# Two more modulation blocks in layer 0's second feed-forward sweep, none in layer 1's recurrent sweeps

## The chip, the cores and the metric

The kernel runs on one core of one Trainium2 chip. The metric is the device time of the whole program in microseconds (us); lower is better. A core has a matrix engine (PE), two elementwise engines (DVE and ACT), GpSimd (POOL) and a queue engine (SP) that here does nothing but start the loads of weights.

## What is computed

One inference step of a two-layer network on 128 context tokens and 128 latent tokens with 2048 channels, everything in float32. Layer 0 mixes by attention, layer 1 by a recurrent block; a feed-forward part (8192 wide, squared ReLU) follows each. Every sub-layer is normalised before and after, and shifted, scaled and gated by values that come from the two condition vectors through one linear map per layer:

```python
def adaln(cond, w, b):
    m = jax.nn.silu(cond) @ w + b
    return [t[:, None, :] for t in jnp.split(m, 6, axis=-1)]
...
    for layer in range(DEPTH):
        shm_p, scm_p, gm_p, shf_p, scf_p, gf_p = adaln(ctx_cond, w_ada[layer], b_ada[layer])
        shm_s, scm_s, gm_s, shf_s, scf_s, gf_s = adaln(c, w_ada[layer], b_ada[layer])
        hp = rmsnorm(yp, g_pre_mix[layer]) * (1 + scm_p) + shm_p
...
        yp = yp + gm_p * rmsnorm(op, g_post_mix[layer])
        hp = rmsnorm(yp, g_pre_ffn[layer]) * (1 + scf_p) + shf_p
...
        yp = yp + gf_p * rmsnorm(ffn(hp, w_ff1[layer], w_ff2[layer]), g_post_ffn[layer])
```

`w_ada` is 2 x 2048 x 12288. In blocks of 512 columns each layer has 24: 0 to 3 the shift and 4 to 7 the scale ahead of the mixer, 8 to 11 the mixer's gate, 12 to 15 the shift and 16 to 19 the scale ahead of the feed-forward part, 20 to 23 its gate. The change is about blocks 12 to 19 of layer 1.

## The kernel before

All weights are streamed once from memory in tiles of 512 rows by 512 columns (1 MB each). There are two kinds of tile. An M tile belongs to one of the big products; ACT and DVE split it into a rounded part (`w_hi`, L776) and the rest (`w_lo`, L1027), in two halves, and PE multiplies both parts with the activations. An A tile belongs to the modulation map; PE takes it as it is (L494, 8 recorded matmuls), and four A tiles make one modulation block.

The work is a list of sweeps (`plan`, L64). Each sweep runs a number of iterations, and each iteration goes through a string of M and A by which SP loads and PE multiplies. Those that matter here: `ff2_0` (layer 0's second feed-forward product) runs 4 iterations of `"MMA" * 4 + "M" * 8`; `rec_in_a` and `rec_in_b` (the recurrent block's input product) and `rec_out` (its output product) run 4 iterations of `"MA" * 4` each; `ff1_1` follows without A tiles. The A tiles of `rec_in_b` and `rec_out` are blocks 12 to 15 and 16 to 19 of layer 1.

All tiles pass through one ring of four slots, `raw`. SP starts the loads strictly in the order of the strings (`tiles`, L361). The load for a position waits until the tile four positions earlier is out of its slot: an M tile is out when DVE has made its `w_lo`, an A tile when PE has multiplied it (`released`, L319).

A modulation block ends in four steps. After its fourth A tile DVE adds the bias, and splits the sum into a short and a long part (`ada_rows_out`: L1061, L1063, L1065); the bank that holds the sum is one for all blocks, so PE's first A tile of the next block waits for this (`ada_row`, in `ada_tile`, L486). Then PE turns the row into columns (L514) or spreads it over the partitions (L518) in `ada_end`, and DVE stores the result (`ada_store`: L1075 for columns, L1079 for a gate). POOL loads each block's bias, and a gate's gain.

In most sweeps (skew) these steps stand in the next iteration: `ada_rows_out` behind the second half of its first M tile. `ff2_0` and `ff2_1` do them within the iteration, `ada_rows_out` behind half 19, which is the tenth M tile's second half, two M tiles after the fourth A tile (halves are numbered from 0: half 19 belongs to the tenth M tile).

In `rec_in_b` the engines do more beside the product. For each of four chunks in an iteration PE computes the recurrence's gates (`rg_gates`, L556), ACT their tanh and exp (L826 to L830), DVE the coefficients and scans (L1324 to L1343); after four chunks ACT takes a square root (L837), ahead of which no scan of these chunks can start. Behind `rec_in_b` DVE finishes the last scans while PE begins `rec_out`, whose fourth M tile needs the last of them.

Of the kernel before, what the change touches and what calls it, by code (L numbers as in the profile page):

```python
# [48 lines left out]
class Sweep:  # L49


    def __init__(self, name, n, mode, weight, col0, tiles, blocks, ada, ada_at, order, out, skew=True):
# [3 lines left out]
        self.ada, self.ada_at = ada, ada_at  # L56
# [4 lines left out]
        assert order.count("M") == tiles * blocks and len(order) % NRAW == 0  # L61


def plan(w):  # L64

    ma = "MA" * 4
    sweeps = [
        Sweep("ada0", 8, None, None, 0, 0, 0, "cols", (0, 0), "AAAA", None),
        Sweep("att_in_a", 4, "token", w["att_in"], 0, 4, 1, "gate", (0, 8), ma, "qkv"),
        Sweep("att_in_b", 5, "token", w["att_in"], 4, 4, 1, "cols", (0, 12), ma, "qkv"),  # L70
        Sweep("att_out_a", 3, "token", w["att_out"], 0, 4, 1, "cols", (0, 17), ma, "op"),
        Sweep("att_out_b", 1, "token", w["att_out"], 3, 4, 1, None, None, "MMMM", "op"),
        Sweep("ff1_0", 8, "feature", w["ff1_0"], 0, 4, 2, "cols", (1, 0), "MMA" * 4, "hidden"),
        Sweep("ff2_0", 4, "token", w["ff2_0"], 0, 16, 1, "gate", (0, 20), "MMA" * 4 + "M" * 8, "op", False),
        Sweep("rec_in_a", 4, "feature", w["rec_in"], 0, 4, 1, "gate", (1, 8), ma, "xr"),
        Sweep("rec_in_b", 4, "feature", w["rec_in"], 4, 4, 1, "cols", (1, 12), ma, "gr"),
        Sweep("rec_out", 4, "token", w["rec_out"], 0, 4, 1, "cols", (1, 16), ma, "op"),
        Sweep("ff1_1", 8, "feature", w["ff1_1"], 0, 4, 2, None, None, "M" * 8, "hidden"),
        Sweep("ff2_1", 4, "token", w["ff2_1"], 0, 16, 1, "gate", (1, 20), "MMA" * 4 + "M" * 8, "op", False),
    ]  # L80
    pos = half = ada = token = feature = gate = main = 0
    for s in sweeps:

        s.pos0, s.main0, s.half0, s.ada0, s.token0, s.feature0, s.gate0 = pos, main, half, ada, token, feature, gate
        pos += s.n * len(s.order)
        main += s.n * s.order.count("M")
        half += s.n * s.halves
        ada += s.n * bool(s.ada)
        gate += s.n * (s.ada == "gate")
        if s.mode == "token":  # L90
            token += s.n * s.blocks
        if s.mode == "feature":
            feature += s.n * s.blocks
    return sweeps


def hybrid_step(nc, A, out):
# [26 lines left out]
    with ctx:  # L124
# [80 lines left out]
        state_rows = rpb[0:2 * KC, 0, :]  # L205
        CONV_W, CONV_B, B_A, B_X, LAM, H0 = 0, 64, 80, 112, 144, 176
# [100 lines left out]
        NORM_ADA = {0: 8, 1: 20, 2: 28, 3: 44}  # L307
# [11 lines left out]
        def released(s, it, p):  # L319


            if p >= NRAW:
                at, upto = (s, it), p - NRAW + 1
            elif first(it):
                k = sweeps.index(s)
                if k == 0:
                    return None
                b = sweeps[k - 1]
                at, upto = (b, b.n - 1), len(b.order) - NRAW + p + 1
            else:  # L330
# [4 lines left out]
            return ada_used, TILE * b.ada0 + i * b.order.count("A") + b.order[:upto].count("A")  # L335
# [23 lines left out]
        @block.sync  # L359
        def _(sp):  # L360
            def tiles(s, it, before):  # L361
                m = a = 0
                for p, kind in enumerate(s.order):
                    if kind == "M":
                        b, t = divmod(m, s.tiles)
                        w, col = s.weight[t], (s.col0 + it * s.blocks + b) * BLK
                        m += 1
                    else:
                        layer, col0 = s.ada_at
                        w, col = W_ada[layer][a], (col0 + it) * BLK  # L370
                        a += 1
                    if not isinstance(it, int):
                        col = sp.snap(col)
                    free = released(s, it, p)
                    if free:
                        sp.wait_ge(*free)
                    sp.dma_start(raw[:, p % NRAW, :, :], w[:, :, bass.ds(col, BLK)]).then_inc(raw_landed[p % NRAW], 16)

            sp.dma_start(stage[0:96, 0, :], A["vectors"][0:96, :]).then_inc(vec_a_landed, 16)
            sp.dma_start(ident[:, :], A["ident"]).then_inc(id_landed, 16)  # L380
            sp.dma_start(sel[:, :], A["sel"]).then_inc(id_landed, 16)
            for s in sweeps:
                iterations(sp, s, tiles, None)
# [3 lines left out]
        def _(pool):  # L387
            def ada_loads(s, it, before):

                b = s.ada0 + it  # L390
                layer, col = s.ada_at
                if not isinstance(b, int) or b > 0:
                    pool.wait_ge(ada_row, b)
                src = A["b_ada"][layer:layer + 1, bass.ds((col + it) * BLK, BLK)]
                pool.dma_start(bias_rows[0:2 * NG, :], src.broadcast_to([2 * NG, BLK])).then_inc(bias_landed, 16)  # L395
                if s.ada == "gate":
                    name = "g_post_ffn" if col >= 20 else "g_post_mix"
                    pool.wait_ge(ada_fin, b)
                    src = A[name][layer:layer + 1, bass.ds(it * BLK, BLK)]
                    pool.dma_start(gain_rows[:, :], src.broadcast_to([P, BLK])).then_inc(gain_landed, 16)  # L400
# [67 lines left out]
            iterations(pool, S["rec_out"], ada_loads, None)  # L468
# [16 lines left out]
        def _(pe):  # L485
            def ada_tile(s, it, p, a):  # L486

                slot, landed = stream(s, it, p)
                b = s.ada0 + it
# [14 lines left out]
            def ada_end(s, it):  # L504

                b = s.ada0 + it
# [5 lines left out]
                if s.ada == "cols":  # L512
# [47 lines left out]
            def body(s, it, before):  # L560
                lanes = NG if s.mode == "token" else BLK // P
                m = a = 0
                for p, kind in enumerate(s.order):
                    if kind == "A":
                        if not (first(it) and p < s.ada_early):
                            ada_tile(s, it, p, a)
                        a += 1
                        if s.mode is None and a == 1 and before and before[0].ada:
                            ada_end(*before)
                        continue  # L570
# [41 lines left out]
                    if m == (3 if s.out == "gr" else 2) and before and before[0].ada and before[0].skew:  # L612
# [133 lines left out]
            ada_end(*last)  # L746
# [3 lines left out]
            ada_end(*last)  # L750
# [262 lines left out]
        def _(dve):  # L1013
# [39 lines left out]
            def ada_rows_out(s, it):  # L1053


                b = s.ada0 + it
# [11 lines left out]
            def ada_store(s, it):  # L1068
                b = s.ada0 + it
                dve.wait_ge(ada_small, b + 1)  # L1070
                if s.ada == "cols":

                    base = s.ada_at[1] - (12 if s.ada_at[1] >= 12 else 0)
                    flat = ada_cols[:, :, :, :].rearrange("p a c g -> p (a c g)")
                    V.tensor_copy(flat[:, bass.ds((base + it) * 4 * NG, 4 * NG)], ps[5][:, 0:4 * NG]).then_inc(ada_fin, 1)  # L1075
# [6 lines left out]
            def body(s, it, before):  # L1082
# [5 lines left out]
                for b in range(s.blocks):  # L1088
                    last = (s, it * s.blocks + b - 1) if b else (before and (before[0], before[1] * before[0].blocks + before[0].blocks - 1))
                    for hh in range(2 * s.tiles):  # L1090
# [22 lines left out]
                        if before and before[0].ada and before[0].skew and b == 0:  # L1113
# [4 lines left out]
                        if not s.skew and hh == 19:  # L1118
                            ada_rows_out(s, it)
                        if not s.skew and hh == 25:  # L1120
                            ada_store(s, it)

            def gate_of(s, blk):

                return {"att_out_a": 12, "att_out_b": 12, "ff2_0": S["ff2_0"].ada0 + blk + 1,
# [41 lines left out]
            def norm(n, gain, ahead, h0):  # L1167
# [3 lines left out]
                steps(V.scalar_tensor_tensor(out=gs, in0=ada_cols[:, 1], scalar=1.0,  # L1171
# [9 lines left out]
                for j in range(KC // 2):  # L1181
# [3 lines left out]
                    for c in range(2):  # L1185
                        for g in range(NG):
                            at = (c * NG + g) * T
                            e = V.tensor_scalar(h_mod[:, j % 2, c, g, :], ps[NORM_BANKS[j % 3]][:, at:at + T],
                                                gs[:, 2 * j + c, g:g + 1], ada_cols[:, 0, 2 * j + c, g:g + 1],
# [239 lines left out]
            ada_rows_out(*last)  # L1429
            split_early("rec_out", 2, 4)  # L1430
            gelu_arguments(3)
            ada_store(*last)
# [14 lines left out]
            ada_rows_out(*last)  # L1447
            dve.wait_ge(states_turned, 1)
            V.tensor_copy(state_rows, ps[6][0:2 * KC, 0:P]).then_inc(state_rows_ready, 1)
            ada_store(*last)  # L1450
# [61 lines left out]
```

## Time and profile before

| | |
|---|---|
| time, 3 runs | median 2509.38 us (2508.92 to 2511.56) |
| span of the profiled execution | 2507.5 us |
| PE busy in it | 2356.4 us (94%) |
| DVE, ACT busy | 1492.8 us (60%), 1107.1 us (44%) |
| SP's loads of weights | 574.77 MB, 65.5% of the 16 DMA engines' span |

The span runs from the first to the last instruction of that execution, so its own time is at least the span; the page gives no more of it. The time on the chip stands some 2 us over it (2509.38 against 2507.5). PE's records overlap, as one matmul starts before the one ahead has drained, so the share of busy time is no measure of how full PE is; better is the distance from one start to the next. The profile's chain of waits follows the run back from its last instruction, at each step to whatever released it, and names the engine and line that the time belongs to.

### The profile page before, as it was taken

The numbers are of one execution on the slowest core, as the hardware profiler recorded it, in microseconds if no ns is written. First come the engines' busy times: TensorE is split into PE (matmuls) and PEld (weight loads), VectorE is DVE, ScalarE is ACT, GpSimd is POOL, SyncE is SP. The second block draws the span as 40 slices with busy tenths as digits, with TensorE's granted clock in tenths as the row PEclk, the third lists the DMA queues.
The fourth block names the chain that finished last, engine by engine and source line by source line (L and its number), as shares of the span: only waits on it lengthen the run. The fifth ranks groups of instructions, "written<-read, shape, count | busy, mean of one in ns | idle before, by whom it ended". The sixth has DMA issues, their size and how long they took to land.

```text
span 2507.5 us, 34322 instructions
## 1 busy us (share of the span) xinstructions
PE 2356.4 (94%) x12179; PEld 1818.1 (73%) x12179; DVE 1492.8 (60%) x2055; ACT 1107.1 (44%) x1529; POOL 85.9 (3%) x139
## 2 busy tenths in 40 slices
PE   5799997989999999999998999897999999999996
PEld 1366765668888887877876777665888888777775
DVE  2444445456555556666767668865655556666665
ACT  0132334334333334555554358733444444555553
POOL 1000000000000000000000011000000000000000
PEclk8799998989999999999999999998999999999998
DMA  9989880765777777666674887687455555766763
GB/s 355 330 299 323 308 316 5 276 227 189 252 251 252 250 251 258 225 250 214 223 251 150 304 285 246 240 284 274 152 189 184 196 186 178 258 220 212 249 218 117
DMA packets 296342, 592.14 MB, mean 236 GB/s; under 512 B 11569, under 2 KB 11825, under 8 KB 296017
## 3 DMA queue, kind: packets, MB, share of 16 engines
q1 hardware_dynamic: 289744, 574.77, 65.5%
q0 software_dynamic: 6528, 16.46, 2.1%
q8 instruction: 42, 0.69, 0.1%
q14 instruction: 28, 0.22, 0.0%
HBM read 587.76 MB, written 3.42 MB: 236 GB/s over the span
## 4 chain that ended last, share of the span: by engine, by line
PE 86%; DMA 5%; DVE 4%; ACT 2%; issue 1%; POOL 1%; DVEq 0%; SPq 0%; ACTq 0%; POOLq 0%
PE bank L539 22%; PE bank L529 15%; PE bank L531 14%; PE bank L530 14%; PE bank L541 11%; PE bank L494 6%; DMA raw<-in_w_ada 3%; PE bank L644 1%; PE bank L556 1%; PE bank L678 1%; DMA raw<-in_w_rec_in 1%; DVE w_lo L1027 1%; DVE x L1154 1%; DMA raw<-in_w_att_in 1%; POOL small L405 0%
## 5 line engine op out<-in xcount | busy, mean ns | idle before, releaser
L1027 DVE TENSOR_TENSOR w_lo<-raw,w_hi 128x1024 fp32r<-128x1024 f32 x712 | 858.0, 1221 | 512.4 <-ACT w_hi L776 511.0
L776 ACT ACTIVATE w_hi<-raw 128x1024 fp32r<-128x1024 f32 x712 | 734.0, 1051 | 725.9 <-DMA raw<-in_w_att_in 217.9
L539 PE MATMUL bank<-xt,w_hi 128*128 128x512 f32 x2560 | 907.5, 399 | 4.0 <-DVE R L1047 2.5
L541 PE MATMUL bank<-xt,w_lo 128*128 128x256 f32 x2560 | 713.4, 279 | 0.0
L529 PE MATMUL bank<-w_hi,xt 128*128 128x512 f32 x1568 | 624.9, 399 | 11.8 <-DVE w_lo L1027 4.1
L531 PE MATMUL bank<-w_hi,xt 128*128 128x512 f32 x1568 | 612.1, 390 | 0.0
L530 PE MATMUL bank<-w_lo,xt 128*128 128x512 f32 x1568 | 611.7, 390 | 0.0
L539 PEld LDWEIGHTS bank<-xt,w_hi 128*128 128x128 f32 x2560 | 480.4, 188 | 159.2 <-issue 31.9
L541 PEld LDWEIGHTS bank<-xt,w_lo 128*128 128x128 f32 x2560 | 481.9, 188 | 0.4
L529 PEld LDWEIGHTS bank<-w_hi,xt 128*128 128x128 f32 x1568 | 294.9, 188 | 150.5 <-issue 66.5
L531 PEld LDWEIGHTS bank<-w_hi,xt 128*128 128x128 f32 x1568 | 295.0, 188 | 63.4
L530 PEld LDWEIGHTS bank<-w_lo,xt 128*128 128x128 f32 x1568 | 295.4, 188 | 58.8 <-issue 0.5
L1025 DVE TENSOR_TENSOR xt<-R,xt 128x512 fp32r<-128x512 f32 x256 | 176.8, 690 | 234.5 <-ACT w_hi L776 234.1
L775 ACT ACTIVATE xt<-R 128x512 fp32r<-128x512 f32 x256 | 161.3, 630 | 315.0 <-PE bank L531 188.0
L494 PE MATMUL bank<-raw,cond 128*32 128x512 f32 x1536 | 225.9, 665 | 31.1 <-DVE ada_rows L1065 16.1
L494 PEld LDWEIGHTS bank<-raw,cond 128*32 128x32 f32 x1536 | 31.9, 112 | 113.2 <-issue 56.8
L812 ACT ACTIVATE R<-bank 128x256 f32 (+1 forms) x160 | 59.8, 381 | 110.3 <-PE bank L541 110.1
L1047 DVE TENSOR_TENSOR R<-bank,R 128x256 f32 (+1 forms) x160 | 65.9, 420 | 33.1 <-ACT R L812 32.7
L395 POOL DMA_DIRECT2D bias_rows<-in_b_ada x48 | 24.6, 513 | 1705.4 <-DVE ada_rows L1065 1705.4
L1061 DVE TENSOR_TENSOR ada_sum<-bank,bias_rows 128x512 f32<-128x512 f32 x48 | 32.9, 686 | 73.0 <-PE bank L494 73.0
L644 PE MATMUL bank<-R,x 128*128 128x128 f32 x256 | 40.8, 323 | 34.3 <-DVE R L1164 34.3
L644 PEld LDWEIGHTS bank<-R,x 128*128 128x128 f32 x256 | 38.7, 237 | 38.6 <-DVE R L1164 25.2
(171 smaller groups left out, 916.1 us busy)
## 6 DMA issues: line engine op xcount, KB each, us to landing
raw<-in_w_ff SPq DMA_DIRECT2D x256, 1024.0 KB, 5.4
raw<-in_w_ada SPq DMA_DIRECT2D x192, 1024.0 KB, 5.6
raw<-in_w_att_in SPq DMA_DIRECT2D x36, 1024.0 KB, 7.0
raw<-in_w_rec_in SPq DMA_DIRECT2D x32, 1024.0 KB, 7.0
raw<-in_w_att_out SPq DMA_DIRECT2D x16, 1024.0 KB, 7.2
raw<-in_w_rec_out SPq DMA_DIRECT2D x16, 1024.0 KB, 7.2
gain_rows<-in_g_post_mix POOLq DMA_DIRECT2D x8, 256.0 KB, 5.0
gain_rows<-in_g_post_ffn POOLq DMA_DIRECT2D x8, 256.0 KB, 4.1
```

What stands on the lines that cost most here:

```text
L494: mm = nc.tensor.matmul(ps[4][32 * j:32 * j + 32, :], cond[:, TILE * a + j, :], raw[:, slot, j, :], start=(a == 0), stop=(a == TILE - 1))
L529: nc.tensor.matmul(o, hi, w_hi[:, h, k, :], start=(begin and k == 0), stop=False)
L530: nc.tensor.matmul(o, hi, w_lo[:, h, k, :], start=False, stop=False)
L531: mm = nc.tensor.matmul(o, lo, w_hi[:, h, k, :], start=False, stop=(end and k == 1))
L539: nc.tensor.matmul(ps[m][:, :], w_hi[:, h, k, m * P:(m + 1) * P], xt[:, c, :], start=(begin and k == 0), stop=False)
L541: mm = nc.tensor.matmul(ps[m][:, 0:NG * T], w_lo[:, h, k, m * P:(m + 1) * P], xt[:, c, 0:NG * T], start=False, stop=(end and k == 1))
L644: mm = nc.tensor.matmul(ps[NORM_BANKS[j % 3]][:, at:at + T], x[:, g, (2 * j + c) * P:(2 * j + c + 1) * P], diag[:, g, :], start=True, stop ...
L775: nc.scalar.activation(xt[:, c:c + 2, 0:NG * T], hidden[:, 2 * h:2 * h + 2, :], ACT.Copy)
L776: nc.scalar.activation(w_hi[:, h % NSPLIT, :, :], raw[:, slot, 2 * q:2 * q + 2, :], ACT.Copy)\
L1025: V.tensor_tensor(xt[:, c:c + 2, NG * T:2 * NG * T], hidden[:, 2 * h:2 * h + 2, :], xt[:, c:c + 2, 0:NG * T].bitcast(fp32), ALU.subtract)
L1027: V.tensor_tensor(w_lo[:, h % NSPLIT, :, :], raw[:, slot, 2 * q:2 * q + 2, :], w_hi[:, h % NSPLIT, :, :].bitcast(fp32), ALU.subtract).then ...
L1047: V.tensor_tensor(dst, ps[m][:, 0:NG * T], dst, ALU.add).then_inc(chunk_read, 1)
```

## The change

A sweep can now have several modulation blocks in an iteration. `ff2_0` gets three: the gate block that it had, then two shift or scale blocks for layer 1's feed-forward part (columns 12, 14, 16, 18 as second and 13, 15, 17, 19 as third block of the four iterations). Its string becomes `"MA" * 8 + "MAA" * 2 + "M" * 6`. `rec_in_b` and `rec_out` lose theirs and become `"MMMM"`. Since layer 1's mixer columns are still in use at that time, the new blocks are stored in the space of `window`, a table that only the attention reads; the norm ahead of `ff1_1` reads them there.

```diff
+        at = [i for i, kind in enumerate(order) if kind == "A"][TILE - 1::TILE]
+        self.ada_after = [order[:i].count("M") for i in at]
...
     ma = "MA" * 4
+    two = "MMA" * 4 + "M" * 8
+    three = "MA" * 8 + "MAA" * 2 + "M" * 6
...
-        Sweep("ff2_0", 4, "token", w["ff2_0"], 0, 16, 1, "gate", (0, 20), "MMA" * 4 + "M" * 8, "op", False),
-        Sweep("rec_in_a", 4, "feature", w["rec_in"], 0, 4, 1, "gate", (1, 8), ma, "xr"),
-        Sweep("rec_in_b", 4, "feature", w["rec_in"], 4, 4, 1, "cols", (1, 12), ma, "gr"),
-        Sweep("rec_out", 4, "token", w["rec_out"], 0, 4, 1, "cols", (1, 16), ma, "op"),
+        Sweep("ff2_0", 4, "token", w["ff2_0"], 0, 16, 1,
+              [("gate", 0, 20, 1), ("cols", 1, 12, 2), ("cols", 1, 13, 2)], three, "op", False),
+        Sweep("rec_in_a", 4, "feature", w["rec_in"], 0, 4, 1, [("gate", 1, 8, 1)], ma, "xr"),
+        Sweep("rec_in_b", 4, "feature", w["rec_in"], 4, 4, 1, [], "MMMM", "gr"),
+        Sweep("rec_out", 4, "token", w["rec_out"], 0, 4, 1, [], "MMMM", "op"),
...
+        ffn_cols = window[:, 0:2 * KC * NG].rearrange("p (a c g) -> p a c g", a=2, g=NG)
...
-        NORM_ADA = {0: 8, 1: 20, 2: 28, 3: 44}
+        NORM_ADA = {0: 8, 1: 20, 2: 28, 3: 40}
...
-                    if not s.skew and m == 11:
-                        ada_end(s, it)
+                    if not s.skew:
+                        for k, after in enumerate(s.ada_after):
+                            if m == after + 3:
+                                ada_end(s, it, k)
...
-                        if not s.skew and hh == 19:
-                            ada_rows_out(s, it)
-                        if not s.skew and hh == 25:
-                            ada_store(s, it)
+                        if not s.skew:
+                            for k, after in enumerate(s.ada_after):
+                                if hh == 2 * after + 3:
+                                    ada_rows_out(s, it, k)
+                                if hh == 2 * after + 9:
+                                    ada_store(s, it, k)
```

On PE the calls of `ada_end` behind `rec_in_b` and behind `rec_out` go, on DVE those of `ada_rows_out` and `ada_store` there, on POOL the bias loads of the two sweeps (`ff2_0` has them instead). For `ff2_0` the rule `ada_after` gives 4, 8 and 10 M tiles, so `ada_rows_out` stands behind halves 11, 19 and 23.

On SP, the queue of loads in `ff2_0`'s first iteration (`in_w_ff` are M tiles, `in_w_ada` A tiles; a load waits for `lo_ready` where an M tile leaves its slot, for `ada_used` where an A tile does). Before, from the iteration's fourth and last A tile to its end:

```order
L377 DMA raw<-in_w_ada 128x4x512 [waits lo_ready]
L377 DMA raw<-in_w_ff 128x4x512 [waits ada_used]
L377 DMA raw<-in_w_ff 128x4x512 [waits lo_ready] x2
L377 DMA raw<-in_w_ff 128x4x512 [waits ada_used]
L377 DMA raw<-in_w_ff 128x4x512 [waits lo_ready] x4
```

With the change, from the ninth M tile to the fourteenth:

```order
L397 DMA raw<-in_w_ff 128x4x512 [waits lo_ready]
L397 DMA raw<-in_w_ada 128x4x512 [waits ada_used]
L397 DMA raw<-in_w_ada 128x4x512 [waits lo_ready]
L397 DMA raw<-in_w_ff 128x4x512 [waits ada_used]
L397 DMA raw<-in_w_ada 128x4x512 [waits lo_ready]
L397 DMA raw<-in_w_ada 128x4x512 [waits ada_used]
L397 DMA raw<-in_w_ff 128x4x512 [waits ada_used]
L397 DMA raw<-in_w_ff 128x4x512 [waits lo_ready]
L397 DMA raw<-in_w_ff 128x4x512 [waits ada_used] x2
```

The first row is the ninth M tile and the fourth row the tenth; the tenth's load now waits until PE has used the A tile four positions earlier, the eighth of the iteration.

On PE, the end of the fifth M tile of `ff2_0`'s first iteration and what follows. Before, the sixth M tile comes at once:

```order
L529 MATMUL bank<-w_hi,xt 128x512
L530 MATMUL bank<-w_lo,xt 128x512
L531 MATMUL bank<-w_hi,xt 128x512
L529 MATMUL bank<-w_hi,xt 128x512 [waits lo_ready]
L530 MATMUL bank<-w_lo,xt 128x512
```

With the change, at the end of the ninth M tile (behind the fifth it reads the same with one A tile in place of two):

```order
L552 MATMUL bank<-w_hi,xt 128x512
L515 MATMUL bank<-raw,cond 32x512 [waits ada_row,raw_landed1]
L515 MATMUL bank<-raw,cond 32x512 x3
L515 MATMUL bank<-raw,cond 32x512 [waits raw_landed2]
L515 MATMUL bank<-raw,cond 32x512 x3
L550 MATMUL bank<-w_hi,xt 128x512 [waits lo_ready]
```

The first A tile of a new block now stands between M tiles and waits for DVE's `ada_row`; the tenth M tile is queued behind it.

On DVE, in the same iteration, what stands ahead of that `ada_row` (the second block's), with the change:

```order
L1046 TENSOR_TENSOR xt<-R,xt 128x2x256 [waits hi_ready]
L1048 TENSOR_TENSOR w_lo<-raw,w_hi 128x1024
L1082 TENSOR_TENSOR ada_sum<-bank,bias_rows 128x512 [waits ada_small,bias_landed,ada_used]
L1084 CAST ada_rows<-ada_sum 128x512 [waits ada_step]
L1086 SCALAR_TENSOR_TENSOR ada_rows<-ada_rows,sel,ada_sum 128x512 [waits ada_step]
```

The first two rows are half 19, the second half of the tenth M tile; the three steps of the row stand behind it, as they did before, where no A tile of the iteration was left to wait for them.

## Rows read from the trace of the kernel before

**Rows 1.** The page: the chain of waits, shares of the span by engine.

```profile
PE 86%; DMA 5%; DVE 4%; ACT 2%; issue 1%; POOL 1%; DVEq 0%; SPq 0%; ACTq 0%; POOLq 0%
```

**Rows 2.** Busy us by stretch: ff2_0, rec_in_b; columns PE PEld DVE ACT POOL, PEclk, DMA, GB/s.

```profile
1068.14:1161.33 93.19, 92.77 (x419) 72.70 (x419) 62.22 (x72) 51.33 (x68) 1.08 (x2) 1.00 0.64 229
1533.95:1571.83 37.88, 34.90 (x198) 26.64 (x197) 32.63 (x60) 30.01 (x50) 6.22 (x9) 1.00 0.72 249
```

**Rows 3.** Chain in ff2_0: start us, us, what; two A tiles in turn.

```profile
1068.21 1.00 PE bank L494 x8
...
1080.32 1.00 PE bank L494 x8
```

**Rows 4.** Chain in rec_out: A tiles in turn, and a block's end.

```profile
1660.27 0.99 PE bank L494 x8
...
1666.94 0.34 PE bank L514 x4
1667.28 0.99 PE bank L494 x8
```

**Rows 5.** SP's queue in rec_out: loads issued at these times.

```profile
1669.38 0.37 SPq L377 DMA_DIRECT2D raw<-in_w_rec_out  x1
1675.16 0.37 SPq L377 DMA_DIRECT2D raw<-in_w_ada  x1
```

**Rows 6.** ACT in rec_out: the splits that wait for those loads.

```profile
1676.38 2.01 ACT L776 ACTIVATE w_hi<-raw 128x1024 fp32r<-128x1024 f32 x2 [5.02 <-DMA raw<-in_w_rec_out]
...
1684.33 2.01 ACT L776 ACTIVATE w_hi<-raw 128x1024 fp32r<-128x1024 f32 x2 [2.83 <-DMA raw<-in_w_rec_out]
```

**Rows 7.** Loads by tensor: KB each, median us from issue to landing.

```profile
raw<-in_w_ff SPq DMA_DIRECT2D x256, 1024.0 KB, 5.4
```

**Rows 8.** ACT in ff2_0: an M tile's split begins when it has landed.

```profile
1005.50 0.63 ACT L775 ACTIVATE xt<-R 128x512 fp32r<-128x512 f32 x1 [4.56 <-DMA raw<-in_w_ff]
```

**Rows 9.** DVE in ff2_0: that tile's two halves, and a block's row.

```profile
1007.73 1.22 DVE L1027 TENSOR_TENSOR w_lo<-raw,w_hi 128x1024 fp32r<-128x1024 f32 x1
...
1009.47 1.21 DVE L1027 TENSOR_TENSOR w_lo<-raw,w_hi 128x1024 fp32r<-128x1024 f32 x1
...
1014.83 0.68 DVE L1061 TENSOR_TENSOR ada_sum<-bank,bias_rows 128x512 f32<-128x512 f32 x1
...
1016.01 0.75 DVE L1065 SCALAR_TENSOR_TENSOR ada_rows<-ada_rows,sel,ada_sum 128x512 fp32r<-128x512 f32 x1
```

**Rows 10.** Chain in an iteration of rec_in_b.

```profile
1544.47 0.43 DVE R L1047
...
1550.86 0.99 PE bank L494 x8
...
1557.67 0.37 ACT R L830
...
1563.08 1.00 PE bank L494 x8
```

**Rows 11.** Chain behind rec_in_b, up to rec_out's fourth M tile.

```profile
1618.76 0.61 DVE ada_sum L1061
...
1620.61 2.27 DVE w_lo L1027 x2
...
1647.88 0.47 PE bank L529
```

**Rows 12.** Chain behind rec_out.

```profile
1735.97 0.69 DVE ada_sum L1061
...
1737.95 0.62 PE bank L514 x4
```

**Rows 13.** PE behind rec_in_b: two waits, and the clock after them.

```profile
1620.66 0.78 PE L514 MATMUL bank<-sel_r,ada_rows 128*128 128x2 f32 x4 [3.01 <-DVE ada_rows L1065]
1624.74 0.79 PE L529 MATMUL bank<-w_hi,xt 128*128 128x512 f32 x1 [3.31 <-DVE xt L1441]
```

**Rows 14.** Busy time and PEclk of the stretch there, columns as in rows 2.

```profile
1620.96:1627.78 6.82, 3.52 (x10) 2.85 (x10) 6.82 (x11) 6.15 (x9) 0.46 (x1) 0.50 0.57 217
```

More of the change, by code:

```diff
@@ L49, with __init__ @@
 class Sweep:
-    def __init__(self, name, n, mode, weight, col0, tiles, blocks, ada, ada_at, order, out, skew=True):
+    def __init__(self, name, n, mode, weight, col0, tiles, blocks, adas, order, out, skew=True):
         self.name, self.n, self.mode = name, n, mode
@@ L60, in __init__ @@
         self.halves = 2 * order.count("M")
-        assert order.count("M") == tiles * blocks and len(order) % NRAW == 0
+        at = [i for i, kind in enumerate(order) if kind == "A"][TILE - 1::TILE]
+        self.ada_after = [order[:i].count("M") for i in at]
+        assert order.count("M") == tiles * blocks and len(order) % NRAW == 0 and len(at) == len(adas)
+        assert len(adas) < 2 or not skew
 def plan(w):
     ma = "MA" * 4
+    two = "MMA" * 4 + "M" * 8
+    three = "MA" * 8 + "MAA" * 2 + "M" * 6
@@ L87, in plan @@
         half += s.n * s.halves
-        ada += s.n * bool(s.ada)
-        gate += s.n * (s.ada == "gate")
+        ada += s.n * len(s.adas)
+        gate += s.n * any(kind == "gate" for kind, *_ in s.adas)
         if s.mode == "token":
@@ L334, in released, with ada_number, ada_block @@
                 return lo_ready, 2 * (b.main0 + i * b.order.count("M") + b.order[:upto].count("M"))
-            return ada_used, TILE * b.ada0 + i * b.order.count("A") + b.order[:upto].count("A")
+            return ada_used, TILE * (b.ada0 + i * len(b.adas)) + b.order[:upto].count("A")
+        def ada_number(s, it, k):
+            return s.ada0 + it * len(s.adas) + k
+        def ada_block(s, it, k):
+            kind, layer, col0, step = s.adas[k]
+            return kind, layer, col0 + it * step
         def iterations(eng, s, body, before):
@@ L388, in ada_loads @@
             def ada_loads(s, it, before):
[L390 to L400, printed above, removed]
+                for k in range(len(s.adas)):
+                    b = ada_number(s, it, k)
+                    kind, layer, col = ada_block(s, it, k)
+                    if not isinstance(b, int) or b > 0:
+                        pool.wait_ge(ada_row, b)
+                    src = A["b_ada"][layer:layer + 1, bass.ds(col * BLK, BLK)]
+                    pool.dma_start(bias_rows[0:2 * NG, :], src.broadcast_to([2 * NG, BLK])).then_inc(bias_landed, 16)
+                    if kind == "gate":
+                        name = "g_post_ffn" if s.adas[k][2] >= 20 else "g_post_mix"
+                        pool.wait_ge(ada_fin, b)
+                        src = A[name][layer:layer + 1, bass.ds(it * BLK, BLK)]
+                        pool.dma_start(gain_rows[:, :], src.broadcast_to([P, BLK])).then_inc(gain_landed, 16)
             def rsqrt(n):
@@ L567, in body @@
                         a += 1
-                        if s.mode is None and a == 1 and before and before[0].ada:
+                        if s.mode is None and a == 1 and before and before[0].adas:
                             ada_end(*before)
@@ L1112, in body @@
                                 outputs(last[1])
[L1113 removed]
+                        if before and before[0].adas and before[0].skew and b == 0:
                             if hh == 1:
```

66 lines of the change are left out of this document (32 added, 34 removed).

## The prediction

> **What bounds the kernel now.** I began with the chain of waits: PE holds 86% of it [rows 1], so a step counts by what it does to PE's start times. The windows say the same by stage. An iteration of `ff2_0` has PE busy for 92.77 of 93.19 us, with nothing else near it; one of `rec_in_b` takes 37.88 with PE at 34.90, DVE 32.63 and ACT 30.01 [rows 2], so there three engines take turns and PE's work is only partly on the path. The change moves 32 A tiles out of the second kind of stage into the first. So three prices are wanted: an A tile in `ff2_0`, an A tile in the recurrent part, and the waits of the new order.
>
> **An A tile on PE.** In `ff2_0`'s old order one period of two M tiles and an A is 1080.32 - 1068.21 = 12.11 us [rows 3]. In `rec_out`, where M and A alternate, the period is 1667.28 - 1660.27 less 0.34 for a block's column end, 6.67 us [rows 4]. The difference gives the M tile, 5.44, and the rest the A tile, 1.23, of which 1.00 is its eight matmuls and the rest the break in the M stream; a second A right behind another costs 1.00.
>
> **Added in `ff2_0`.** An iteration goes from four breaks to ten and from 4 A tiles to 12. Six more breaks at 1.23, two adjacent A tiles at 1.00 and two column ends at 0.34 are 10.1 us; times four, **+40.2**. Nothing hides it, since PE is full there. DVE's two more rows (1014.83 to 1016.76, 1.93 us each [rows 9]) and the stores cost nothing by themselves: PE's 92.77 there stand against DVE's 62.22 [rows 2]. The bias loads on POOL wait for the previous block's row, tens of us ahead of their use. SP issues the same number of loads; M and A in turn at 6.67 is a rate that `rec_out` already sustains [rows 4].
>
> **The new waits in `ff2_0`.** There is one sum bank, so PE's first A tile of a block waits until DVE has made the row of the block before. DVE does this behind the second half of the second M tile after that block's last A tile. In the old order no A of the iteration was left to wait. Now the next block's first A stands one M tile behind, and DVE's row stands behind the split of an M tile that PE does not even need yet. How late is it? A tile's split starts when it has landed; DVE has its first half ready 3.45 us later (1005.50 to 1008.95) and the second 5.18 later (1010.68) [rows 8, 9]; the row adds 1.93. And the loads go in order, each when the tile four positions ahead has left its slot:
>
> - Fifth M tile. The sixth's load follows the A load that waits for PE's third A. In `rec_out` the same succession, A done at 1668.27, M load issued at 1669.38, split started at 1676.38 [rows 4, 5, 6], takes 8.1. The row comes at 8.1 + 5.18 + 1.93 = 15.2 behind the end of the third A; PE is there after an M, an A and an M (5.67 + 1.00 + 5.67, where 5.67 is a period of 6.67 less 1.00) = 12.3. **Wait 2.9.**
> - Ninth M tile. The tenth's load waits for PE's use of the eighth A. It is issued some 0.2 later (an estimate, from SP's 0.37 for a load [rows 5]) and lands in 5.4, the median for `in_w_ff` [rows 7]. The row comes at 0.2 + 5.4 + 5.18 + 1.93 = 12.7, PE at 5.67. **Wait 7.1.**
> - Eleventh M tile itself. It is loaded behind the use of the ninth A and shares the queue with A loads: 8.1 + 3.45 = 11.5 against two A tiles and an M, 8.7. **Wait 2.8.**
>
> That is 12.8 an iteration, **+51.2**. For the landing, 5.4 is the low end, 9.2 the high one (issued 1675.16, split started 1684.33 [rows 5, 6], an A load with its M load behind). I take 8.1 where an A load goes ahead, 5.4 where none does. With 9.2 at the first and third, and 8.1 at the second, the sum is 17.7 an iteration (+71); with 5.4 everywhere the first and third waits are 0.2 and 0.1, and it is 7.4 (+30).
>
> The Trainium skill's "DMA: Bandwidth & Descriptors", section "Anatomy of one DMA — SWDGE (gpsimd) path", gives a transfer as 2.0 us and its bytes at 436 GB/s, an estimated 4.4 us for one of these tiles; it is fitted on another issuing path, and by it only the second wait would be left, some 6 us, and the time would be near 2548. The trace's medians and landings are longer, so they are used.
>
> **The clock.** Where PE had waited 3.01 and 3.31 us behind `rec_in_b`, the granted clock was 0.50 (1.2 GHz) until 1627.78, 3.0 us after PE had resumed at 1624.74 [rows 13, 14]: half of that, 1.5 us, was lost. `ff2_0`'s clock is now 1.00 throughout [rows 2]. Part of what a slower M tile loses is taken out of the next wait. I take 0.7 us an iteration, **+2.8**; bounds 0 and 1.5 at each of three waits, 18 in all.
>
> **Saved in `rec_in_b`.** The chain there goes through four M tiles, but also through DVE's L1047 and ACT's L830 [rows 10]; only two of an iteration's four A tiles are on it. 2 x 1.23 x 4 = **-9.8**. Bounds: 0, if ACT or DVE carry the iteration, and four A tiles and a column end, 5.3 x 4 = 21.
>
> **Saved in `rec_out`.** Its start loses DVE's row, 1618.76 to 1620.61 on the chain: **-1.9**. Its first three A tiles lie beside DVE's scans, for which PE waits until its fourth M tile at 1647.88 [rows 11]; they save nothing. From then to the last M tile, twelve A tiles at 1.23 and three column ends at 0.34 go, 15.8, less an estimated 1.3 for waits on banks at block ends that the A tiles now cover: **-14.5**. The sixteenth lies beside the closing of the last block. Behind the sweep the row and its columns go, 1735.97 to 1738.57 [rows 12]: **-2.6**. The saving is 28.8, with bounds 19 and 41.
>
> **The sum.** 40.2 + 51.2 + 2.8 - 28.8 = +65.4. On the profiled span of 2507.5 that is 2572.9; the median of the runs stands 1.9 above the span, so **2575 us**. With its own bounds 2554 (waits 30) to 2603 (waits 71, and 8 more of clock).
>
> **Rivals.**
> - *The rows come in time.* If tiles land and DVE runs ahead further than the landings of `rec_out` tell, no first A waits: 2509.4 + 40.2 - 28.8 = 2521. For it: `ff2_0` loads at 229 GB/s before [rows 2], so there is bandwidth to spare. Against it: a lead of four slots ties the loads to PE's own uses, whatever the bandwidth. Chance 0.12 (2510 to 2535).
> - *The recurrent part gains most, and the change is faster.* There DVE is the next bound: 32.63 less one row and its store (2.1, estimate from rows 9) is 30.5, so an iteration could lose 7.4 us, 29.5 in all [rows 2, 9]. With 19.0 in `rec_out`, and no waits, 2509.4 + 40.2 - 48.5 = 2501. It decides only if the waits stay under 2 us an iteration. The Trainium skill's "Perfetto Trace Analysis", section "Optimization Strategy", says that interleaving regimes with different busiest engines may improve the time; that is this move. Against it stands the trace: ACT and DVE are already on that chain between PE's tiles [rows 10]. Chance 0.05.
> - *Worse.* The loads behind a wait come late too, the low clock follows each wait and `rec_in_b` gives nothing: +40 + 71 + 8 - 19 = 2610. Chance 0.09 (2603 to 2625).
>
> **How the numbers follow.** The forecast has 0.74 and most of that within its own bounds. To hold 8 in 10 the range takes in the first rival's middle below and reaches a little over the forecast's high end: 2520 to 2606. A difference of 0.2%, 5 us, is about what a measurement of this kernel can tell from none. Faster: the second rival, 0.05. Within 0.2%: the low ends of the first rival, 0.04. Slower: the rest, 0.91. A rival in which the change does nothing isn't there: the same number of tiles goes through, and PE's order differs in every iteration of three sweeps.
>
> **What would show it.** Right: in `ff2_0` PE waits for DVE's row (its third step) at eight first A tiles, four times some 3 us and four times some 7, and four times about 3 at the eleventh M tile; an iteration takes 93.2 + 10.1 + 12.8 + 0.7 = 117 us; one of `rec_in_b` 35.4; a group of four M tiles in `rec_out` 21.8 in place of 27.0; stretches of clock 0.50 inside `ff2_0`. Wrong: `ff2_0` near 103 (no waits) or over 125, or `rec_in_b` under 32 or unchanged.

## The result and the profile after

The changed kernel takes 2600.37 us (median of 4 runs, 2597.94 to 2602.09) against 2509.71 for the kernel before: 1.0362 times as long, 95% interval 1.0349 to 1.0375. The forecast was 2575 with a range of 2520 to 2606. Direction and mechanism came out as argued; of +65.4 us forecast, +90.7 came, and most of the missing 25 lie in one term, the clock.

To see where they lie, take the start of PE's first M tile in each sweep, in both traces. A sweep's length is the distance to the next sweep's start.

| sweep | before, us | after, us | difference | forecast |
|---|---|---|---|---|
| `att_in_a` to `ff1_0` | 850.0 | 848.8 | -1.2 | 0 |
| `ff2_0` | 390.3 | 507.1 | +116.8 | +94.2 |
| `rec_in_a` | 115.4 | 115.0 | -0.4 | 0 |
| `rec_in_b` | 155.4 | 144.9 | -10.5 | -9.8 and the -1.9 at its end |
| `rec_out` | 130.7 | 117.5 | -13.2 | -14.5 and the -2.6 at its end |
| `ff1_1`, `ff2_1` | 752.1 | 752.0 | -0.1 | 0 |

Windows of the trace after: `ff2_0`'s second iteration; three stretches in it that begin where PE has just waited; an iteration of `rec_in_b`; a group of `rec_out` (columns as in rows 2).

```profile
1087.00:1208.28 121.28, 108.67 (x492) 77.25 (x491) 65.19 (x79) 50.51 (x68) 2.07 (x4) 0.93 0.71 245
1122.64:1130.90 8.26, 8.26 (x32) 5.36 (x32) 3.56 (x4) 3.04 (x4) 0.50 (x1) 0.79 0.66 228
1158.76:1168.74 9.98, 9.98 (x40) 5.58 (x40) 0.00 (x0) 0.00 (x0) 0.50 (x1) 0.74 0.69 237
1172.77:1179.95 7.18, 7.18 (x25) 5.74 (x25) 5.16 (x6) 4.07 (x6) 0.00 (x0) 0.76 1.04 390
1619.41:1654.89 35.48, 30.11 (x161) 25.51 (x161) 30.64 (x56) 30.02 (x50) 5.81 (x9) 1.00 0.46 148
1774.00:1796.50 22.50, 22.08 (x98) 17.95 (x97) 11.11 (x11) 9.64 (x12) 0.00 (x0) 1.00 0.55 187
```

The first line answers to `ff2_0`'s line in [rows 2]: 121.28 us in place of 93.19, PE no longer full (108.67), the mean granted clock 0.93 in place of 1.00. The next three tell why the clock is lower; more on them below. `rec_in_b`'s iteration went from 37.88 to 35.48, `rec_out`'s group from 27.0 to 22.5.

The view of waits, PE in `ff2_0` after the change (total us, times, longest):

```profile
PE bank L515 <- DVE ada_rows L1086: 42.6, 8, 7.3
PE bank L550 <- DVE w_lo L1048: 12.6, 4, 4.7
```

The eight first A tiles and the four eleventh M tiles of the forecast are there, by name and by count; in `ff2_0` before, PE had neither wait. The chain of waits in the second iteration shows each of the three (start us, us, what):

```profile
1108.43 7.03 DMA raw<-in_w_ff
...
1116.10 1.05 ACT w_hi L797
...
1119.52 1.22 DVE w_lo L1048
1120.74 0.61 DVE ada_sum L1082
...
1121.84 0.76 DVE ada_rows L1086
1122.64 1.68 PE bank L515 x8
...
1145.98 5.60 DMA raw<-in_w_ff
...
1155.63 1.22 DVE w_lo L1048
1156.85 0.61 DVE ada_sum L1082
...
1158.76 3.69 PE bank L515 x16
1162.59 6.58 DMA raw<-in_w_ff
...
1171.49 1.23 DVE w_lo L1048
1172.77 0.50 PE bank L550
```

Read it downwards. The sixth M tile's load lands, ACT and DVE split it, and only then comes the row (`ada_sum`, `ada_rows`) that PE's first A tile wants; PE starts it at 1122.64, 2.77 us after it had run dry (in brackets the idle time ahead and what ended it):

```profile
1122.64 0.83 PE L515 MATMUL bank<-raw,cond 128*32 128x512 f32 x4 [2.77 <-DVE ada_rows L1086]
```

The same again with the tenth M tile, up to 1158.76, after 7.32 us. Then the eleventh M tile, loaded when PE had used the two A tiles behind the ninth M tile: up to 1172.77, after 2.10 us. A single A tile takes 1.68 in that chain and a pair 3.69, against 1.00 for a single one in [rows 3]. PE ran at the lower of its two clock levels there, 1.2 GHz: the granted clock was 0.54 from 1122.64 to 1126.30 and 0.50 from 1158.76 to 1162.33.

### The profile page after: what moved, and what is told of

Same layout as the page of the kernel before. It is cut to its first block, busy times and chain, and to the rows that moved or that the text cites. A ratio compares the mean times of both kernels' runs of the same rounds, so it can differ in the third digit from the quotient of the medians.

```text
span 2599.1 us, 34309 instructions
## 1 busy us (share of the span) xinstructions
PE 2386.0 (92%) x12179; PEld 1832.7 (71%) x12179; DVE 1490.7 (57%) x2055; ACT 1104.5 (42%) x1529; POOL 85.8 (3%) x139
## 4 chain that ended last, share of the span: by engine, by line
PE 47%; DVE 5%; DMA 3%; ACT 2%; issue 2%; POOL 0%; DVEq 0%; ACTq 0%; SPq 0%
PE bank L560 12%; PE bank L550 9%; PE bank L552 8%; PE bank L551 8%; PE bank L562 6%; DMA raw<-in_w_ff 3%; PE bank L515 2%; DVE w_lo L1048 1%; ACT w_hi L797 1%; DMA raw<-in_w_rec_in 1%; PE bank L667 1%; PE bank L577 1%; DVE x L1179 1%; DVE R L1364 0%; ACT R L850 0%
## 5 line engine op out<-in xcount | busy, mean ns | idle before, releaser
L550 PE MATMUL bank<-w_hi,xt 128*128 128x512 f32 x1568 | 634.4, 405 | 30.8 <-DVE w_lo L1048 19.6
L552 PE MATMUL bank<-w_hi,xt 128*128 128x512 f32 x1568 | 617.6, 394 | 0.0
L550 PEld LDWEIGHTS bank<-w_hi,xt 128*128 128x128 f32 x1568 | 298.9, 191 | 184.0 <-issue 67.1
L552 PEld LDWEIGHTS bank<-w_hi,xt 128*128 128x128 f32 x1568 | 298.6, 190 | 65.2
L515 PE MATMUL bank<-raw,cond 128*32 128x512 f32 x1536 | 233.8, 691 | 72.5 <-DVE ada_rows L1086 58.7
```

The lines of the kernel that those rows point to most:

```text
L515: mm = nc.tensor.matmul(ps[4][32 * j:32 * j + 32, :], cond[:, TILE * a + j, :], raw[:, slot, j, :], start=(a == 0), stop=(a == TILE - 1))
L550: nc.tensor.matmul(o, hi, w_hi[:, h, k, :], start=(begin and k == 0), stop=False)
L552: mm = nc.tensor.matmul(o, lo, w_hi[:, h, k, :], start=False, stop=(end and k == 1))
```

## The experiments

The kernels ran on different chips, each beside the kernel before on the same one (its medians there: 2511.20, 2513.61 and 2509.60), so ratios are compared.

**Is it the row, or the loads?** The rows of all three blocks one M tile earlier:

```diff
-                                if hh == 2 * after + 3:
+                                if hh == 2 * after + 1:
                                     ada_rows_out(s, it, k)
```

> DVE makes each block's row behind the second half of the first M tile after the block's last A tile, not of the second. Theory (the row is late because it stands behind the split of an M tile that PE does not need yet): the waits of PE's first A tiles for the row, 15.0 and 27.6 us over four iterations, go; the tenth M tile, whose load still waits for the eighth A tile, is then some 1.7 us late (ready 9.35 us after that A tile, wanted at 7.6), and the eleventh stays 2 to 3 us late. Waits 55.3 to about 17, the low clock behind them from 21 to about 10: 2551 us (2540 to 2562), ff2_0 iterations near 109 in place of 121. Rival (the loads are what is late, the row wait only covers for it): the same time shows up as waits of the sixth and tenth M tile for their split, 2590 to 2600.

Measured: 2564.51 us, ratio 1.0202 (1.0179 to 1.0224). All waits of PE for a row are gone from `ff2_0`, but the time is 13 over the forecast. Its iterations take 112, not 109, and PE now waits for splits of M tiles:

```profile
PE bank L550 <- DVE w_lo L1048: 29.2, 13, 3.9
```

What is in the way shows on DVE (start us, us, engine, line):

```profile
1151.26 1.22 DVE L1048 TENSOR_TENSOR w_lo<-raw,w_hi 128x1024 fp32r<-128x1024 f32 x1
1156.98 0.69 DVE L1082 TENSOR_TENSOR ada_sum<-bank,bias_rows 128x512 f32<-128x512 f32 x1 [4.50 <-PE bank L535]
```

The third block's row needs the buffer that PE empties with the second block's column end (L535), and PE does this only after its eleventh M tile. DVE stands 4.50 us, the splits behind it stand too, and PE waits 3.84 us for one of them, the twelfth M tile's. The step was moved past a wait of its own. So the third row alone was put back:

```diff
-                                if hh == 2 * after + 3:
+                                if hh == 2 * after + (1 if k < 2 else 3):
                                     ada_rows_out(s, it, k)
```

> The early row for the first two blocks of an iteration alone; the third block's row stays where the change has it. In the run with all three rows early DVE stood 4.50 us in the third row, waiting for PE's column end of the second block, and the thirteenth M tile's split came 3.84 us late for PE. Theory (an early row pays only where PE's matmul ahead of it is done): that wait goes, with the clock behind it, 5 us an iteration: 2564 - 20 = 2544 us (2538 to 2550), as with two banks. Rival (the time lies with the loads): no change from 2564.

Measured: 2543.73 us, ratio 1.0123 (1.0108 to 1.0139), as expected.

**The same wait taken away on the other side.** DVE's order stays, and the second block of an iteration sums in a free bank:

```diff
-                    pe.wait_ge(ada_row, b)
+                    pe.wait_ge(ada_row, b - 1 if k else b)
                 for j in range(TILE):
-                    mm = nc.tensor.matmul(ps[4][...
+                    mm = nc.tensor.matmul(ps[7 if k == 1 else 4][...
...
-                V.tensor_tensor(ada_sum[:, :], ps[4][...
+                V.tensor_tensor(ada_sum[:, :], ps[7 if k == 1 else 4][...
```

> The middle block of an iteration sums in a bank of its own, and PE's first A tile of the second and third block waits only for the row of the block before the last. DVE's order is that of the change. Theory (one bank and one late row make the wait): no first A tile waits in ff2_0; the tenth M tile is some 1.7 us late and the eleventh 2 to 3: 2551 us (2540 to 2562), the same as with the early row. Rival (loads late): 2590 to 2600. Rival (DVE itself is the bound there): slower than the early row by 5 us or more.

Measured: 2540.50 us, ratio 1.0106 (1.0083 to 1.0129): better than expected, with an interval that overlaps that of the two early rows. `ff2_0` before and in this trace:

```profile
963.60:1353.90 390.30, 378.34 (x1725) 296.78 (x1725) 261.08 (x309) 210.42 (x280) 8.57 (x12) 0.99 0.66 231
964.20:1411.60 447.40, 422.89 (x2013) 307.19 (x2013) 273.43 (x341) 207.11 (x280) 12.56 (x20) 0.98 0.80 277
```

Of the two groups of waits that the change had there, PE's waits for a row are gone and these are left:

```profile
PE bank L550 <- DVE w_lo L1048: 12.8, 8, 2.2
```

Two different remedies for the late row each give back some 60 us (1.0362 down to 1.0106 and 1.0123). That the row was late is thereby shown; the rival that the loads were late in any case (2590 to 2600) is out. What is left over `ff2_0` before is 447.4 - 390.3 = 57.1, of which 40.2 is the price of the tiles by the prediction and 12.8 are waits for splits, all but one of them at the tenth and eleventh M tiles and none over 2.2.

**What does the clock cost?** Matmuls that nobody reads were put ahead of the three waits, so that PE is busy while it waits:

```diff
+            def fill(n):
+                for _ in range(n):
+                    nc.tensor.matmul(ps[7][0:32, :], cond[:, 0, :], cond[:, :, :].rearrange(...), ...)
...
+                if a == 0 and k:
+                    fill((10, 26)[k - 1])
...
+                        if s.name == "ff2_0" and h == 20:
+                            fill(8)
```

> The change, with matmuls whose result nobody reads ahead of each of the three waits in ff2_0: 10 (2.5 us) ahead of the second block's first A tile, 26 (6.5 us) ahead of the third's, 8 (2.0 us) ahead of the eleventh M tile, each a little shorter than the wait. The row and the loads come no earlier, so the waits stay as filled time. If the low clock behind each wait costs what I now read (116.8 added, less 40.2 for the tiles and 55.3 of waits, 21 us): the clock stays at 1.00 and the time is about 2581 us (2577 to 2586). If the clock's loss is made good in the next wait, as the prediction had it: within 4 us of 2600. If the fill delays the loads behind it: above 2602.

Measured: 2675.74 us, ratio 1.0649 (1.0627 to 1.0671). This one missed, since the fill was sized wrongly. Its line in the trace (records; ns of one, min/median/max; first and last start) and `ff2_0`'s window:

```profile
L529 PE MATMUL bank<-cond x352: 592/592/617, 993.9 to 1490.5; 128*32 128x512 f32 x176
```

```profile
961.30:1543.80 582.50, 570.81 (x2365) 344.78 (x2365) 274.00 (x344) 207.14 (x280) 12.56 (x20) 0.99 0.62 213
```

I had taken 0.25 us for one from the A tile's 1.00 for four; ten of them took 8.3 us. So the fill outlasted the waits, PE waited for no row at all, and the clock is 0.99. It shows that the low clock goes with the idle time, but not its price. With sizes from that trace:

```diff
-                    fill((10, 26)[k - 1])
+                    fill((3, 7)[k - 1])
...
-                            fill(8)
+                            fill(2)
```

> As the run before with matmuls ahead of the three waits, but sized by what they took there (0.83 us each, 18.9 records' worth of 8.3 us for ten): 3, 7 and 2 of them, 2.5, 5.8 and 1.7 us, under waits of 2.8 to 6.2, 6.7 to 7.3 and 2.1 to 4.7. If the low clock behind the waits costs 4 to 5 us an iteration: the granted clock stays at 1.00 in ff2_0 and the time is about 2600 - 18 = 2582 us (2577 to 2588). If the clock's loss is made good in the waits that follow: within 4 us of 2600.

Measured: 2584.37 us, ratio 1.0284 (1.0268 to 1.0299). Where 1.0362 stood for the change, 0.8% or 20 us are gone, though nothing comes earlier and PE does more. One iteration of it:

```profile
1081.90:1199.99 118.09, 113.51 (x514) 77.06 (x514) 65.19 (x79) 50.51 (x69) 2.07 (x4) 1.00 0.72 252
```

The clock is 1.00 in place of 0.93. Over `ff2_0` the fill is 4 x 12 x 0.83 = 40 us, and 14.2 of waits for the row and the eleventh tile are left:

```profile
PE bank L517 <- DVE ada_rows L1094: 7.9, 7, 3.2
PE bank L556 <- DVE w_lo L1056: 6.3, 4, 1.7
```

Together that is 54, about the 55.2 of waits in the change, yet `ff2_0` takes 490.7 instead of 507.1. So the low clock's price there is some 15 to 16 us. The 20 of the whole time holds more than that: in this trace `att_in_b`, where nothing was changed, is 3.4 shorter than in the change's.

**What does the recurrent part give by itself?** The change without its additions to `ff2_0`. This leaves blocks 12 to 19 of layer 1 out altogether and takes the mixer's values in their place, so the outputs are not the network's; only the time is of use:

```diff
-              [("gate", 0, 20, 1), ("cols", 1, 12, 2), ("cols", 1, 13, 2)], three, "op", False),
+              [("gate", 0, 20, 1)], two, "op", False),
...
-                mod = ffn_cols if n == 3 else ada_cols
+                mod = ada_cols
```

> The removal alone: blocks 12 to 19 of layer 1 are in no sweep, so layer 1's feed-forward part is modulated by the mixer's values in their place; ff2_0 is as it was before. If the recurrent part gains by itself what the trace of the change shows by stage (10.5 in rec_in_b, 13.2 in rec_out, 0.4 in rec_in_a, against 0.4 lost earlier and 1.3 gained in ff1_0): about 2509.7 - 24 = 2485 us. By the prediction's terms 28.8 less: 2481. If the gain of the stages hung on what went ahead of them: over 2490.

Measured: 2488.69 us, ratio 0.9909 (0.9887 to 0.9932), so 17 to 28 us under its kernel before; in the trace `rec_in_b` takes 143.3 and `rec_out` 117.1, within 2 us of the change. The gain of the recurrent part does not depend on `ff2_0`, and the two sides may be added.

**The order that needs no row early.** Two M tiles between a block's end and the next block's first A tile, and fewer breaks:

```diff
-    three = "MA" * 8 + "MAA" * 2 + "M" * 6
+    three = "MMAA" * 6 + "M" * 4
...
-                                if hh == 2 * after + 9:
+                                if hh == min(2 * after + 9, s.halves - 1):
```

> The change with ff2_0's string as MMAA six times and then MMMM, DVE's order by the same rule. The same tiles in six breaks rather than ten, and between the end of a block and the next block's first A tile lie two M tiles, not one. Theory (a first A tile waits because it is asked for one M tile behind the block's end): from the second A tile's use to the wanted row PE has four M and two A tiles, 24 us, and the row takes about 18, so no row waits; a pair costs 2.23, so ff2_0 gains 9.2 us an iteration over the kernel before: 2511 + 36.7 - 24 = 2522 us (2515 to 2532). Rival (two adjacent A tiles by themselves starve the M tile behind them, as the eleventh tile's wait of 2 to 3 us suggested): each of 24 pairs costs some 2 us more and the clock some 1.4, 2600 us.

Measured: 2525.90 us, ratio 1.0050 (1.0035 to 1.0065). No first A tile waits; PE's only new waits in `ff2_0`:

```profile
PE bank L550 <- DVE w_lo L1048: 8.2, 10, 1.8
```

So pairs by themselves hardly starve the M tile behind them: ten waits behind 24 pairs, 0.8 us each. `ff2_0` takes 434.2, 43.9 more than before, where tiles (36.7) and waits (8.2) make 44.9. Of 3.6% lost by the change 3.1 were the order within one sweep. The rest is the price of the tiles, less what the recurrent part gives.

**Pairs in the kernel before.** If a break in the M stream costs something, it is to be saved without any move (`ma` is the string of six sweeps; the last two lines stand for `ff2_0` and `ff2_1`):

```diff
-    ma = "MA" * 4
+    ma = "MMAA" * 2
...
-        ... "cols", (1, 0), "MMA" * 4, "hidden"),
+        ... "cols", (1, 0), "MMAAMMMMAAMM", "hidden"),
-        ... "MMA" * 4 + "M" * 8, ...
+        ... "MMMMAA" * 2 + "M" * 8, ...
```

> The kernel before, with its A tiles in pairs: MA four times becomes MMAA twice, MMA four times becomes MMAAMMMMAAMM in ff1_0 and MMMMAA twice in ff2_0 and ff2_1. Nothing changes place between sweeps. If the break in the M stream costs 0.23 us as read from the periods (1.23 for a single A tile, 1.00 for one behind another): 80 breaks fewer, of which those in rec_in_b and at the start of rec_out lie off the path, some 65 x 0.23 = 15 us less: 2496 us (2490 to 2504). Rival (an A tile costs the same wherever it stands): 2511. Rival (pairs starve the M tile behind them): slower than before.

Measured: 2505.04 us, ratio 0.9969 (0.9957 to 0.9982), half of what was expected. By stage it gained in `att_in_b` (-5.8), `ff1_0` (-4.9), `ff2_0` (-2.2) and `ff2_1` (-2.7), and lost in `att_in_a` (+2.7), `att_out_a` (+3.3), `rec_out` (+7.3) and, with no A tile in it, `ff1_1` (+6.6). The profiled execution was one of the slowest of this kernel (2510.91 us), so the stages do not add up to the median's gain. In three of the six sweeps where every second tile is an A tile pairs cost time: in `rec_out` ACT's splits sat idle 9.23 us until a load landed, against 5.02 in [rows 6]. Why the other three, with the same string, did not suffer is open.

```profile
1657.64 2.00 ACT L776 ACTIVATE w_hi<-raw 128x1024 fp32r<-128x1024 f32 x2 [9.23 <-DMA raw<-in_w_rec_out]
```

Then pairs only where they paid, and (its edit is not shown) the change with the order `"MMAA" * 6 + "M" * 4` and the same pairs:

```diff
-        Sweep("att_in_b", ... (0, 12), ma, "qkv"),
+        Sweep("att_in_b", ... (0, 12), "MMAA" * 2, "qkv"),
-        Sweep("ff1_0", ... "MMA" * 4, "hidden"),
+        Sweep("ff1_0", ... "MMAAMMMMAAMM", "hidden"),
-        Sweep("ff2_0", ... "MMA" * 4 + "M" * 8, "op", False),
+        Sweep("ff2_0", ... "MMMMAA" * 2 + "M" * 8, "op", False),
-        Sweep("ff2_1", ... "MMA" * 4 + "M" * 8, "op", False),
+        Sweep("ff2_1", ... "MMMMAA" * 2 + "M" * 8, "op", False),
```

> The kernel before with A tiles in pairs only where the run with pairs everywhere gained by stage: att_in_b (-5.8 there), ff1_0 (-4.9), ff2_0 (-2.2), ff2_1 (-2.7); att_in_a, att_out_a, the recurrent sweeps stay in single tiles (pairs lost 2.7, 3.3 and, in rec_out, 7.3 there). Theory (pairs pay where at least two M tiles run between A tiles and the ring is ahead): some 12 to 16 us under the kernel before, 2498 us on a chip where that takes 2512 (2494 to 2503). The 6.6 us that ff1_1 lost with pairs, where there is no A tile, should be gone if they came from the sweeps ahead; if they come from this order of loads, they stay and the time is about 2505. Rival (the stage gains were chance): no change from before.

> The change at its best: ff2_0 as MMAA six times and MMMM, and pairs in att_in_b, ff1_0 and ff2_1 as in the run beside it. If the prices add up (2526 with MMAA alone, less some 5 in ff1_0, 3 in ff2_1, 3 to 6 in att_in_b): about 2514 us (2509 to 2519), no better than the kernel before and some 15 us behind the same pairs without the move. If the move had a gain that only the order hid: under 2500.

Measured: 2494.28 us, ratio 0.9934 (0.9915 to 0.9953), for the kernel before with pairs, which is faster than both kernels of this case; and 2515.91, ratio 1.0018 (1.0004 to 1.0031), for the move with its best order so far and the same pairs. The move itself, in that order, costs some 20 us. A pair on the chain in `ff2_0` of the faster one:

```profile
1069.18 1.85 PE bank L494 x16
1071.04 0.43 PE bank L529
```

1.85 for two A tiles, where two single ones have 1.00 each [rows 3], and one break fewer. That a break costs PE time is shown: in all three traces with pairs `ff1_0` (-4.4 to -4.9) and `ff2_1` (-2.7) gained, and `ff2_0` in the two where its order is otherwise that of before (-2.2 and -2.5). In the faster kernel the four stages' gains add to 14.2 of the 15.0 us between the two spans. Some of it is no gain of the pairs: `att_in_b` gave 4.6, but its three inner iterations went from 27.0 to 26.3 each, and the length of its first varied between 28.3 and 33.3 us in runs where it was unchanged.

## Why the prediction was right, and where it was off

**PE is the bound in `ff2_0`, and nothing hides an A tile there** (+40.2): right. In the run with two banks what is left of the sweep's growth after its waits is 57.1 - 12.8 = 44.3, with some low clock (0.98, against 0.99 before) in it.

**The three waits** (2.9, 7.1, 2.8 an iteration; +51.2): right in place, cause and nearly in size. Measured over the four iterations are 15.0, 27.6 and 12.6, in all 55.2. The second iteration alone reads 2.77, 7.32 and 2.10. The first wait is longer in the first iteration (6.17); why is open. In the third wait two words of the forecast were wrong without changing its number: the load waits for the tenth A tile, 1.00 behind the ninth, and the 8.7 are an M tile and three A tiles, not two. The landing times taken from `rec_out` held: the chain above has 7.03, 5.60 and 6.58 us for the three loads, against 7.0 (1669.38 to 1676.38 [rows 5, 6]), 5.4 [rows 7] and again 7.0. An estimate of 4.4 by the Trainium skill's "DMA: Bandwidth & Descriptors", "Anatomy of one DMA — SWDGE (gpsimd) path", would have been too short here, as was its 2548.

**The clock** (+2.8): this is the step that failed: "Part of what a slower M tile loses is taken out of the next wait. I take 0.7 us an iteration". What is left of +116.8 after the tiles and the waits is 116.8 - 40.2 - 55.2 = 21.4 us, or 5.3 an iteration, and the filled waits gave 15 to 16 of it back; the other 5 to 6 have no experiment of their own. The three windows show it: 8.26 us for an A and an M tile where 6.67 is the period [rows 4], so 1.6 lost; 9.98 for two A tiles and an M where 7.7 would do (1.23 + 1.00 + 5.44), so 2.3; 7.18 where an M tile starts 5.44 to 5.7 later, so 1.5. That is 5.4. My own upper bound, 1.5 at each wait and 18 in all, was near it; I chose the low side on an argument, that later waits absorb the loss, which no row supported. The waits show little sign of it: the second and third of an iteration follow slow stretches, and are 6.7 to 7.3 and 2.1 to 4.7 us long, against 7.1 and 2.8 forecast at full clock. A likely reason, argued and not tested by itself: the row is late by PE's own uses of earlier tiles, so a PE that is slower asks for its next loads later, too. The Trainium skill's "TensorE: Matmul & The Clock Gate", section "HAM oscillation — how this bites in real kernels", describes a kernel that pays the low clock again in every tile because it waits in every tile; this trace agrees, with 0.79, 0.74 and 0.76 behind three successive waits.

**The recurrent part** (-28.8): measured 24.1 in the three sweeps. `rec_in_b` came out as forecast, 10.5 against 11.7 with its end: its last iteration, at whose end DVE's row stood, went from 41.9 to 37.8, the one shown above only from 37.88 to 35.48. `rec_out` gave 13.2 where 17.1 were forecast. A group of four M tiles in it takes 22.5 instead of the 21.8 that I gave, and the first group grew, from 29.8 to 31.1. Its fourth M tile still comes 23.1 us behind the first (1729.60 to 1752.72, as 1624.74 to 1647.88 before [rows 11, 13]), since DVE's scans end when they did. PE, with no A tiles to run meanwhile, now waits 4.47 us where it had waited 1.68, and pays the clock behind it: 7.96 us for this M tile at a granted clock of 0.68, where 6.65 at 1.00 had held an M and an A tile:

```profile
1752.72 0.77 PE L550 MATMUL bank<-w_hi,xt 128*128 128x512 f32 x1 [4.47 <-DVE w_lo L1048]
```

So the three A tiles there were free, as I had said, and besides kept PE's wait short and its clock up behind it, which I had not. By the two profiled spans (+91.6) 26.2 us are missing: 18.6 are the clock's (by what is left over in `ff2_0`), 4.0 the waits', 4.7 the recurrent part's, less 1.2 by which the sweeps ahead of `ff2_0` are shorter.

**The rivals.** "The rows come in time" (2521) is what the better order gives: 2525.9, a forecast of the move nearly without its waits (8.2 left), though by another order with cheaper tiles (36.7). "The recurrent part gains most" is out: an iteration of `rec_in_b` lost 2.4 us, not 7.4. Faster than before was reached by no order that was tried: with no row late and with the best pairs, the move stays 0.2% above. The Trainium skill's advice to interleave regimes ("Perfetto Trace Analysis", "Optimization Strategy") is meant for kernels in which the most-contended engine changes from one regime to the next. Here PE is the busiest engine in both [rows 2], and no run shows a gain from the move.

## What to carry to other kernels

Before a step is moved, ask of each of its handshakes not only how long it takes but behind what it is queued: DVE's row took 1.9 us and was 7 us late, because it stood behind the split of a tile whose load waited for PE itself. A wait of a matmul engine at full clock is to be priced with the slow stretch behind it, here 1.5 to 2.3 us on waits of 2 to 7 us, every time and not once. And where a bound engine pays for each change between two kinds of tile, put like tiles side by side, as far as the ring's lead allows: the kernel with pairs was 0.7% faster, where the move lost 3.6%.

## What was not expected of the hardware

- The clock fell behind waits as short as 2.10 us, and not at once. The granted clock was 1.00 up to that wait (1168.74 to 1172.77); of the M tile that began at 1172.77 the first six matmuls ran at nearly full pace (0.23 to 0.33 us apart), then eight slower (seven 0.42 to 0.43 us apart), from 1174.3 to 1177.7, where the granted clock was 0.52, with PE busy throughout.
- Four matmuls of an A tile take 1.00 us together, while ten fill matmuls of the same shape took 8.3. The A tile's go to four different groups of 32 output rows, the fill's all to one. What separates them was not tried further.
- In two profiled runs (all pairs; the move with pairs) `ff1_1`, whose code and order are unchanged, took 366.5 us instead of 360.0, with PE full and the clock shown as 1.00; `ff1_1` took 359.9 in the others. The orders of both differ from before by pairs, but so does the fastest one's, which took 359.9. What makes it stays open; both profiled executions lay some 6 us over the median of their kernel (2510.91 against 2505.04, 2522.38 against 2515.91), so it looks like a spread that single executions can have, and not like a price of the orders.
